# The FFN's hidden values turned by DMAs and VectorE's 32x32 transposes, two blocks at a time

## The reference, cut to what matters

```python
h2 = _rms_norm(x, norm_ffn)
gate, up = jnp.split(h2 @ w_gate_up, 2, axis=-1)      # (256, 1024) @ (1024, 5632)
return x + (jax.nn.silu(gate) * up) @ w_down          # (256, 2816) @ (2816, 1024)
```

## Time and profile before

| | |
|---|---|
| median of 3 runs | 808.48 us |
| the profiled execution | 808.65 us, of which the span is 806.9 us |
| PE busy | 801.1 us, 99% (3872 matmuls) |
| DVE busy, ACT busy, POOL busy | 68%, 50%, 8% |
| DMA engines, mean busy share for the SP queue | 54.7% |

### The profile page before, as it was taken

One profiled execution on the slowest core, in us unless ns is written; L12 is line 12 of the kernel. 1 busy time (PEld: TensorE's weight loads), 2 busy tenths in 40 slices (PEclk: granted clock), 3 DMA queues, 4 the chain that ended last, 5 costly groups with the idle time before them and its releaser, 6 DMA issues.

```text
span 806.9 us, 10253 instructions
## 1 busy us (share of the span) xinstructions
PE 801.1 (99%) x3872; PEld 658.3 (82%) x3872; DVE 551.6 (68%) x808; ACT 406.1 (50%) x561; POOL 68.1 (8%) x121
## 2 busy tenths in 40 slices
PE   8999999999999999999999999999999999999998
PEld 7788788778888888888888877888788888888886
DVE  7788888867586544665578778799575754565444
ACT  6865646454364343443376656555543543444431
POOL 5944000000000000000006100000000000000000
PEclk9999999999999999999999999999999999999999
DMA  8654546456456645656574625464446555656541
GB/s 313 201 189 144 171 134 231 160 159 201 140 177 211 206 157 193 201 182 207 136 253 121 222 79 190 161 223 161 152 157 209 195 169 180 206 188 205 161 157 52
DMA packets 99553, 144.38 MB, mean 179 GB/s; under 512 B 11689, under 2 KB 62641, under 8 KB 99505
## 3 DMA queue, kind: packets, MB, share of 16 engines
q1 hardware_dynamic: 99504, 143.73, 54.7%
HBM read 142.54 MB, written 1.05 MB: 178 GB/s over the span
## 4 chain that ended last, share of the span: by engine, by line
PE 95%; POOL 3%; DMA 1%; SPq 0%; DVE 0%; issue 0%; POOLq 0%; DVEq 0%
PE big L1599 19%; PE big L1603 19%; PE big L1602 19%; PE mix L1603 10%; PE mix L1599 10%; PE mix L1602 10%; PE mix L1985 1%; PE mix L1643 1%; PE mix L1742 1%; PE mix L1667 1%; DMA pos_i<-in_positions 1%; PE mix L1655 1%; POOL logits L697 1%; PE mix L1689 1%; PE mix L1724 1%; POOL pool_b L743 0%
## 5 line engine op out<-in xcount | busy, mean ns | idle before, releaser
L788 ACT ACTIVATE w_hi<-w_raw 128x2048 fp32r<-128x2048 f32 (+2 forms) x140 | 255.0, 1827 | 165.8 <-DMA w_raw<-in_w_gate_up 86.9
L1107 DVE TENSOR_TENSOR w_lo<-w_raw,w_hi 128x2048 fp32r<-128x2048 f32 (+3 forms) x142 | 305.3, 2164 | 31.7 <-ACT w_hi L788 29.6
L1599 PE MATMUL big<-w_hi,act_hi 128*128 128x512 f32 (+2 forms) x476 | 184.2, 387 | 0.0
L1603 PE MATMUL big<-w_hi,act_lo 128*128 128x512 f32 (+2 forms) x476 | 181.5, 381 | 0.0
L1602 PE MATMUL big<-w_lo,act_hi 128*128 128x512 f32 (+2 forms) x476 | 181.4, 381 | 0.0
L1599 PE MATMUL mix<-w_hi,act_hi 128*128 128x512 f32 x352 | 137.4, 390 | 0.0
L1603 PE MATMUL mix<-w_hi,act_lo 128*128 128x512 f32 x352 | 137.1, 389 | 0.0
L1602 PE MATMUL mix<-w_lo,act_hi 128*128 128x512 f32 x352 | 136.9, 389 | 0.0
L1599 PEld LDWEIGHTS big<-w_hi,act_hi 128*128 128x128 f32 x476 | 89.5, 188 | 18.8 <-issue 1.9
L1385 DVE TENSOR_TENSOR y_h_lo<-mix,y_h_hi 128x256 fp32r<-128x256 f32 x44 | 16.6, 420 | 127.3 <-ACT y_h_hi L1018 127.3
L1603 PEld LDWEIGHTS big<-w_hi,act_lo 128*128 128x128 f32 x476 | 89.5, 188 | 17.1
(11 more groups left out here) (214 smaller groups left out, 721.1 us busy)
## 6 DMA issues: line engine op xcount, KB each, us to landing
w_raw<-in_w_in SPq DMA_DIRECT2D x44, 1024.0 KB, 5.2
w_raw<-in_w_gate_up SPq DMA_DIRECT2D x88, 512.0 KB, 4.8
w_raw<-in_w_down SPq DMA_DIRECT2D x22, 1024.0 KB, 4.8
w_raw<-in_w_o SPq DMA_DIRECT2D x8, 1024.0 KB, 5.0
w_raw<-in_b_w_out SPq DMA_DIRECT2D x4, 1024.0 KB, 6.0
w_raw<-in_w_in SPq DMA_DIRECT2D x4, 512.0 KB, 3.8
w_raw<-in_a_w_out SPq DMA_DIRECT2D x4, 512.0 KB, 4.0
w_raw<-in_d_w_out SPq DMA_DIRECT2D x4, 512.0 KB, 4.3
```

What stands on the lines that cost most here:

```text
L788: nc.scalar.activation(high(u)[:, a:b], arrived(u)[:, a:b], ACT.Copy).then_inc(hi_ready, 1)
L1107: nc.vector.tensor_tensor(low(u)[:, a:b], arrived(u)[:, a:b], high(u)[:, a:b].bitcast(F32), ALU.subtract).then_inc(lo_ready, 1)
L1599: ins = nc.tensor.matmul(dst[:, 0:w], xh, wh, start=first and n == 0, stop=False)
L1603: ins = nc.tensor.matmul(dst[:, 0:w], xl, wh, start=False, stop=end)
```

## The change

The transposes of blocks 0 to 9 leave PE. Two blocks (2j, 2j+1) form pair j (five pairs in a layer); block 10 is alone and is turned by PE as before (`turn_last`).

- `hidden` writes its result into half of `merged` (free in the FFN), with four groups of 32 columns apart, so that what one DMA moves is 128 values in a row. Its second operation (256 columns) becomes two of 128.
- `move_pair`: SP issues 16 DMAs for a pair. Each moves 32 partitions x 2 token blocks x 128 values (512 bytes in a row, 32 KB in all) from `merged` to a quarter of the partitions of `probs` (also free). The first eight stand behind the load of slot MOVE_AT+4 and wait until `hidden` of both blocks is done and the pair before has been turned; the other eight stand behind the load of slot MOVE_AT+5. MOVE_AT[j] is the slot behind the two gate-up units of block 2j+1.
- `turn_pair`, DVE, slot MOVE_AT+3, ahead of that slot's split: waits for all 16 moves, then two transposes of 128x512 (each turns 32x32 squares) from `probs` to `probs_t`.
- ACT takes the high part and DVE the low part of a pair in one operation of 128x512 per tb, from SBUF, in slot MOVE_AT+4 (pairs 0 and 4) or MOVE_AT+5 (pairs 1 to 3). From pair 1 on, ACT also waits until the down unit before the pair is released.
- The list of units is gu0 to gu4, dn0, dn1, gu5, gu6, dn2, dn3, gu7, gu8, dn4, dn5, gu9, gu10, dn6, dn7, dn10, dn8, dn9. Block 10's values go through `y_ac_hi` and `y_ac_lo`.

```diff
@@ plan_units, main
     for f in range(NF):
         add(("gu", f), [("gu", f, 0, h) for h in range(2)])
-        if f >= 2:
-            add(("dn", f - 2), [("dn", f - 2, 0, 0)])
-    for f in (NF - 2, NF - 1):
-        add(("dn", f), [("dn", f, 0, 0)])
+        if f >= 4 and f % 2 == 0:
+            for g in pair_of(f // 2 - 2):
+                add(("dn", g), [("dn", g, 0, 0)])
+    for g in DOWN_LAST:
+        add(("dn", g), [("dn", g, 0, 0)])
@@ slots
-        HID_AT = {0: AT["gu", 1], 1: AT["gu", 2], **{f: DN[f - 2] for f in range(2, NF)}}
-        EVICT_AT = {0: AT["gu", 1] + 1, **{f: DN[f - 1] for f in range(1, NF)}}
+        HID_AT = {f: SLOT[FIRST["gu", f] + 2] for f in range(NF)}
+        MOVE_AT = {j: HID_AT[2 * j + 1] for j in range(LAST)}
+        TURN_AT = {j: MOVE_AT[j] + 3 for j in range(LAST)}
+        EVICT_AT = {j: MOVE_AT[j] + (5 if 0 < j < LAST - 1 else 4) for j in range(LAST)}
+        EVICT_AT[LAST] = DN[NF - 1] - 1
+        STEPS_FIRST += [EVICT_AT[LAST - 1], EVICT_AT[LAST]]
@@ block.sync
+            def move_pair(l, j, quarters):
+                if quarters[0] == 0:
+                    for f in pair_of(j):
+                        for tb in range(TB):
+                            sp.wait_ge(*mix_is_drained(l, "gu", f, tb))
+                    if j > 0:
+                        sp.wait_ge(*hid_turned.nth(l, TB * j))
+                for a in quarters:
+                    for b in range(QUARTERS):
+                        c0 = N * (j % 2) + P * b
+                        sp.dma_start(hid_by_value[quarter(b), :, a, :], merged[quarter(a), :, c0:c0 + P]
+                                     ).then_inc(hid_moved.sem, 16)
...
+                    for j in range(LAST):
+                        for half in range(2):
+                            if SLOT[u] == MOVE_AT[j] + RING - 1 + half:
+                                move_pair(l, j, range(2 * half, 2 * half + 2))
@@ block.scalar
+                for j in range(LAST):
+                    if s == EVICT_AT[j]:
+                        if j > 0:
+                            act.wait_ge(*place_free.nth(l, RING + FIRST["dn", 2 * j - 1] + 1))
+                        for tb in range(TB):
+                            act.wait_ge(*hid_turned.nth(l, TB * j + tb + 1))
+                            nc.scalar.activation(y_h_hi[:, :, tok(tb)], hid_t[:, tb], ACT.Copy).then_inc(hid_hi.sem, 1)
@@ block.vector, hidden
-                nc.vector.scalar_tensor_tensor(out=h, in0=h, scalar=ffn_scale[:, tb:tb + 1], in1=mix[:, bank, FC:2 * FC],
-                                               op0=ALU.mult, op1=ALU.mult).then_inc(mix_drained[bank].sem, 1)
+                for k in range(2):
+                    part = slice(k * P, (k + 1) * P)
+                    ins = nc.vector.scalar_tensor_tensor(out=hidden_at(f, k, tb), in0=by_quarters(h[:, part]),
+                                                         scalar=ffn_scale[:, tb:tb + 1],
+                                                         in1=by_quarters(mix[:, bank, FC + k * P:FC + (k + 1) * P]),
+                                                         op0=ALU.mult, op1=ALU.mult)
+                ins.then_inc(mix_drained[bank].sem, 1)
+            def turn_pair(l, j):
+                dve.wait_ge(*hid_moved.nth(l, 16 * MOVES * (j + 1)))
+                for tb in range(TB):
+                    nc.vector.transpose(hid_t[:, tb].rearrange("p k (a q) -> p k a q", a=QUARTERS),
+                                        hid_by_value[:, tb].rearrange("p a (k c) -> p k a c", k=4)
+                                        ).then_inc(hid_turned.sem, 1)
+            def hidden_low(l, j, tb):
+                dve.wait_ge(*hid_hi.nth(l, TB * j + tb + 1))
+                nc.vector.tensor_tensor(y_h_lo[:, :, tok(tb)], hid_t[:, tb], y_h_hi[:, :, tok(tb)].bitcast(F32),
+                                        ALU.subtract).then_inc(hid_lo.sem, 1)
@@ block.tensor
                     gate_up(l, f, 0)
-                    if f == 1:
-                        turn_hidden(l, 0)
                     gate_up(l, f, 1)
-                    if f > 1:
-                        turn_hidden(l, f - 1)
-                    if f >= 2:
-                        down(l, f - 2)
-                turn_hidden(l, NF - 1)
-                down(l, NF - 2, [0])
-                down(l, NF - 1, [0])
-                down(l, NF - 2, [1])
+                    if f == NF - 1:
+                        down(l, NF - 5)
+                        turn_last(l)
+                        down(l, NF - 4)
+                    elif f >= 4 and f % 2 == 0:
+                        for g in pair_of(f // 2 - 2):
+                            down(l, g)
+                first, second = DOWN_LAST[1:]
+                down(l, DOWN_LAST[0])
+                down(l, first, [0])
+                down(l, second, [0])
+                down(l, first, [1])
                 if l + 1 < DEPTH:
                     turn(l + 1, "hT", 0)
-                down(l, NF - 1, [1])
+                down(l, second, [1])
```

More of the change, by code:

```diff
@@ L53, with pair_of @@
 OUT_K = {"A": 2, "B": 4, "C": 2, "D": 2}
+PAIRS = -(-NF // 2)
+def pair_of(j):
+    return range(2 * j, min(2 * j + 2, NF))
+LAST = PAIRS - 1
+assert len(pair_of(LAST)) == 1
+DOWN_LAST = [NF - 1, NF - 3, NF - 2]
 def plan_units():
@@ L205 @@
 DVE_STEPS = 116
+QUARTER = 32
+QUARTERS = P // QUARTER
+MOVES = QUARTERS * QUARTERS
 class Signal:
@@ L1013, in steps @@
                     high_gained(l, "h2T", 0)
-                for f in range(NF):
[L1015 to L1020, removed]
+                for j in range(LAST):
[5 more added lines that the diff above has]
+                            nc.scalar.activation(y_h_hi[:, :, tok(tb)], hid_t[:, tb], ACT.Copy).then_inc(hid_hi.sem, 1)
+                if s == EVICT_AT[LAST]:
+                    for tb in range(TB):
+                        y_high(l, y_ac_hi[:, :, tok(tb)], 1.0, "hid", tb, n=FC).then_inc(last_hi.sem, 1)
+                for f in range(NF):
                     if s == HID_AT[f]:
@@ L1387, in hidden_low, with last_low @@
+            def last_low(l, tb):
+                bank = mix_bank("hid", tb)
+                dve.wait_ge(*last_hi.nth(l, tb + 1))
+                nc.vector.tensor_tensor(y_ac_lo[:, :, tok(tb)], mix[:, bank, 0:FC].rearrange("p (k t) -> p k t", k=2),
+                                        y_ac_hi[:, :, tok(tb)].bitcast(F32), ALU.subtract
                                         ).then_inc(mix_drained[bank].sem, 1)
@@ L1511, in steps @@
                             hidden(l, f, tb)
+                for j in range(LAST):
+                    if s == TURN_AT[j]:
+                        turn_pair(l, j)
             for l in range(DEPTH):
@@ L1969, in gate_up @@
                         releases = set()
-                        if tb == 0 and h == 0 and f in (0, 1, 2):
+                        if tb == 0 and h == 0 and UNITS[unit - 1][0] != "dn":
                             releases = {-1}
@@ L1990, in down @@
                     unit = FIRST["dn", f]
+                    hi, lo, k0 = (y_ac_hi, y_ac_lo, 0) if f == NF - 1 else (y_h_hi, y_h_lo, 2 * (f % 2))
                     for tb in blocks:
-                        pe.wait_ge(*mix_is_drained(l, "hid", f, tb))
+                        pe.wait_ge(*(mix_is_drained(l, "hid", tb) if f == NF - 1 else
+                                     hid_lo.nth(l, TB * (f // 2) + tb + 1)))
                         for c in range(2):
                             releases = set()
-                            if (tb, c) == (0, 0) and f < NF - 2:
+                            if (tb, c) == (0, 0) and UNITS[unit - 1][0] != "dn":
                                 releases = {-1}
-                            if (tb, c) == (1, 1) and f < NF - 1:
+                            if (tb, c) == (1, 1) and f != DOWN_LAST[-1]:
                                 releases = releases | {1}
-                            parts = [(unit, 2 * k + c, 2 * (f % 2) + k) for k in range(2)]
-                            segment(l, ("dn", c, tb), parts, tb, y_h_hi, y_h_lo, releases, first=f == 0,
-                                    last=f == NF - 1)
+                            parts = [(unit, 2 * k + c, k0 + k) for k in range(2)]
+                            segment(l, ("dn", c, tb), parts, tb, hi, lo, releases, first=f == 0,
+                                    last=f == DOWN_LAST[-1])
                 gate_up(l, 0, 0, (0,))
```

56 lines of the change are left out of this document (35 added, 21 removed).

## The result

The changed kernel takes **798.64 us** (median of four runs, 797.89 to 799.19), the kernel before 808.44 beside it (808.06 to 810.18): a ratio of 0.987, 95% interval 0.986 to 0.989. The kernel is faster, by about 9.8 us where I worked out 8.9.

A forecast was written before the change was run, and what follows sets the result against it. PE's issue list was taken to bound the FFN. Profiled 808.65 us minus 8.9 for 20 transpose groups, plus 0 for hidden added work, gave 799.75; allowing 0.17 for the median, it said 799.7 us, range 799.0 to 804.0.

The forecast's parts named there:

- The mechanism: FFN: PE is limited by what it issues; removed transposes save 8.9 us, all added work stays hidden; chance 0.79.
- What the removed work is worth: PE, FFN: four transposes cost 0.447 us between neighbouring matmuls; 20 groups removed save 8.9 us.
- The check by the period: PE: a block takes 16.81 us, 72 matmuls 16.32, leaving 0.48 for a transpose group and its change-overs.
- The price of a transpose: PE queue: 0.11 us per transpose; the skill's 390 ns would make 80 of them 31 us.
- SP's moves: SP issues a move every 0.62 us; t = 0 is when PE begins the block after the pair.
- Landing: Moves land 4.6 us after issue, taken from v_mid; the last, issued at t = 13.5, at 18.1.
- my 2.7: Pairs 0 to 3: split behind the turn done at t = 21.8, wanted at 24.5; smallest margin, 2.7 us.
- The 960 us: Skill-based estimate: if 2 us fixed per DMA added up for 16 moves, the kernel would be near 960 us.
- No change: Rival: PE makes up the removed work itself, 5.6 ns more pitch per FFN matmul; about 808.5 us, chance 0.04.
- partly hidden: Rival: a 3.03 us load issue behind moves makes the split 0.3 us late for 8 pairs; 802.1 us, chance 0.08.
- The slower case: Rival: moves issue too slowly, PE waits before second gate-up unit and dn8; 852 us at 1.29 pitch, chance 0.09.
- Its formula: Slower rival: with move pitch p, PE waits from p = 0.91 on, by 15p - 13.7 us per pair.

The follow-up runs named there:

- twice: Kernel before the change, with each of its 88 transposes issued twice, in groups of eight: 818.10 us, ratio 1.012.
- evict5: Changed kernel (16 moves per pair), with the high and low parts of pair 0 taken one slot later: 799.61 us, ratio 0.988.
- moves24: Changed kernel with half of the moves cut in two by token block, 24 DMAs per pair, same bytes: 819.24 us, ratio 1.013.
- turn8: Changed kernel with eight more unread DVE transposes of 128x512 per pair, ahead of the two that count: 818.4 us, single run.
- moves32: Changed kernel with every move cut in two by token block, 32 DMAs of 16 KB per pair, same bytes: 864.60 us, ratio 1.069.
- sizes: Changed kernel with 20 idle groups of 1, 2, 4, 8 and 16 transposes in turn before down units: 813.69 us, single run.
- short4: Changed kernel with 20 idle groups of four ordinary 128-column float32r matmuls in front of down units: 808.09 us, single run.
- moves24_first: Changed kernel, 24 moves per pair, pair 0's parts one slot later, block 3's tanh ahead of that slot's split on ACT: 809.68 us, ratio 1.0019.

## Why the prediction was nearly right, and where it failed

**The mechanism held.** PE's list bounds the FFN, 20 groups left it, and all that was added lies beside it. idle4 shows it from the other side: put 20 groups of four transposes back that do nothing, and all the time is back.

**The step that failed is the size of a group.** Under "What the removed work is worth" I measured it between the matmuls at 304.77 and 305.67 and got 0.447. The check by the period, in the same paragraph, gave 0.48, and I called the rest "change-overs" and did not count it. It counts: 20 x 0.484 = 9.7 against 8.9. In the profiled execution's terms that is 808.65 - 9.7 = 798.95, with 799.06 measured. There is a slip in the sum too: 799.75 less the 0.17 between the profiled execution and the median is 799.6, not the 799.7 that I wrote. With both put right the sum is 798.8, beside the 798.64 measured; as it stood, the measured time fell below the range. The rows for it were in the trace of before. Further behind the group its timeline has:

```profile
308.21 0.39 PE L1599 MATMUL big<-w_hi,y_h_hi 128*128 128x512 f32 x1
```

From 305.67 to 308.21 are 11 matmuls in 2.54 us, 0.231 each and not 0.2267: 0.047 us that the two neighbours don't show. 0.447 + 0.047 = 0.494 there; over two blocks it is 0.484. I gave the 0.48 a place as the lower end of the range (799.0), when it was the better reading of the two and belonged in the sum. The remaining tenth or two is below the scatter of the runs.

**The price of a transpose.** The pitch of 0.11 us was right (0.107 in twice). The Trainium skill's 390 ns (VectorE: DVE Perf Modes, section "The three transpose paths"; the figure is for bf16, these are float32) is not what a transpose takes from PE's queue in a stream: 80 of them, with what a group adds, were worth 9.7 us.

**SP's moves.** 0.62 apart predicted, 0.64 measured; first eight from t = 1.9 to 7.1 (predicted 1.6 to 6.6), the load behind them at 8.4 (8.2), last eight done at 14.5 (14.1). Landing was 2.8 us in the median, and not the 4.6 of v_mid; the last move of pair 0 landed in less than 1.9 (its issue begins at 256.9, DVE starts at 258.79). That is most of the difference between the margin of 5.3 and my 2.7. The 960 us that the prediction estimated by the Trainium skill did not come. The 2 us per DMA stand there (DMA: Bandwidth & Descriptors, section "Anatomy of one DMA") for DMAs issued from GpSimd, and these are issued from SP; eight of them go out in 5.1 us.

**DVE.** A transpose of 128x512 took 0.686, predicted 0.69 from another operation of that width. DVE is busy 570.7 us (about 575). The split behind a turn was done at t = 19.2, predicted 21.8.

**A step I overlooked.** I followed a pair to its split and stopped there. The parts of pair 0 stand ahead of `hidden` of block 3, behind a unit that loads late, so pair 1 starts at t = 3.8 and not at 1.6. In the changed kernel that costs nothing (evict5). It accounts for 9.6 of the 20.6 us that moves24 lost where I expected none, and it made turn8's wait at pair 1 twice what I expected.

**The rivals.** No change, and partly hidden, are out by the period of 32.64 us. A load right behind eight moves took 0.53 us at most to issue, and a move 1.41, where the second of them reckoned with 3.03. The slower case is out for this kernel, but its place was right: moves32 waits just there. Its formula was not. It prices the wait by the last landing of one pair, and has neither the lateness that pair 0 hands to pair 1 nor the half clock after a wait.

## What to carry to other kernels

Price what leaves a full PE by the period of the repeating block, and not by the two neighbours of what leaves; where the two readings differ, the period decides. When a step is made later but stays hidden, follow it through the lists of the other engines to the next iteration's start, since lateness is handed on there before it reaches the engine that bounds. Here a wait of PE of 5.3 us cost 7.8: the period that holds it is 40.40 in place of 32.64.

## What the runs showed of the hardware

- Behind a group of 1 to 16 transposes two to nine of the following 512-column matmuls start a few ns late (up to 9), 0.01 to 0.05 us in all, and this does not grow with the group (before, sizes). Behind four ordinary 128-column matmuls it is mostly two, 0.01 us in all (short4). Why is open.
- In this stream one more float32 transpose of 128x128 in a row costs 0.107 us (twice), and one alone 0.160 us (sizes).
- A DMA issue on SP takes 0.59 us for a move of 32 KB and of 16 KB alike. DMAs from SBUF to SBUF landed in 2.8 us (32 KB, 16 per pair) and 1.8 us (32 per pair), where v_mid's of 32 KB took 4.6.
- After a wait of 5.3 us PE ran ten matmuls at the lower clock, 0.43 us apart (moves24). After waits of 3.4 us in turn8 it fell once (0.56 in the window behind it) and once it did not (1.00); the six waits of at most 2.3 us in moves24_first left it at 1.00.
